# A hybrid decoder step on one core: scores ahead of values, and modulation inside the projections

## The reference, cut to what matters

```python
mod = (silu(c) @ w_ada + b_ada).reshape(B, 6, 1, 1024)          # shift1, scale1, gate1, shift2, scale2, gate2
h = x * (1 + scale1) + shift1
qa, ka, va, qb, kb, vb = split(h @ w_in)                        # six blocks of 512 columns
# rope on q and k; mixer A: 8 heads x 64, dilated windows; mixer B: 4 heads, two maps of 64, values of 128
oa = attend_a(qa, ka, va)                                       # sample: 2048 window rows + 8 new
ob = rms_norm(attend_b(qb, kb, vb, lam), subln_g) * 0.8         # sample: 16 pages of 128 rows + 8 new
x = layer_norm(alpha * x + gate1 * (concat(oa, ob) @ w_o), ...)
h = x * (1 + scale2) + shift2                                   # gated ConvFFN, second layer norm
```

## Time and profile before

| | |
|---|---|
| median of three runs | 1229.12 us |
| lowest and highest | 1226.54 and 1235.38 us |
| the profiled execution | 1233.46 us |
| span of its instructions | 1231.5 us |
| mean granted TensorE clock | 0.923 |
| bytes moved | 276.54 MB |

### The profile page before, as it was taken

One profiled execution on the slowest core, in us unless ns is written; L12 is line 12 of the kernel. 1 busy time (PEld: TensorE's weight loads), 2 busy tenths in 40 slices (PEclk: granted clock), 3 DMA queues, 4 the chain that ended last, 5 costly groups with the idle time before them and its releaser, 6 DMA issues.

```text
span 1231.5 us, 23995 instructions
## 1 busy us (share of the span) xinstructions
PE 1052.7 (85%) x9389; PEld 854.0 (69%) x9389; DVE 839.2 (68%) x1513; ACT 269.5 (22%) x580; POOL 357.9 (29%) x379
## 2 busy tenths in 40 slices
PE   5599999999578677677776996999999999999994
PEld 3377777666455555455555775999999999677772
DVE  1657457167676767667659467567676687998958
ACT  0310010132132223322242104332233222100002
POOL 2333233100000000000016005456565665433323
PEclk9699999999888889778786997999999999999997
DMA  8959895596899999999990215475567731413102
GB/s 303 399 171 327 300 353 174 187 331 220 279 351 344 316 367 322 360 313 343 333 322 1 64 53 195 143 265 207 205 244 274 264 105 69 149 58 106 70 17 77
DMA packets 112549, 276.54 MB, mean 225 GB/s; under 512 B 9608, under 2 KB 33174, under 8 KB 108837
## 3 DMA queue, kind: packets, MB, share of 16 engines
q1 hardware_dynamic: 99125, 250.82, 58.6%
q10 hardware_dynamic: 13312, 24.19, 5.5%
HBM read 264.60 MB, written 76.69 MB: 277 GB/s over the span
## 4 chain that ended last, share of the span: by engine, by line
PE 60%; DVE 18%; DMA 7%; SPq 7%; issue 4%; POOL 2%; ACT 2%; ACTq 0%; DVEq 0%; POOLq 0%; PEldq 0%
PE wide L1576 16%; PE wide L1578 15%; PE wide L1577 15%; DVE ring L1151 3%; PE wide L1650 2%; DMA ring<-in_cache_k 2%; DMA ring<-in_w_ada 2%; PE wide L1639 2%; PE wide L1701 2%; PE wide L1732 2%; DVE ring_r L1083 2%; SPq L598 2%; SPq L433 1%; PE wide L1525 1%; DMA ring<-in_w_down 1%
## 5 line engine op out<-in xcount | busy, mean ns | idle before, releaser
L747 POOL TENSOR_TENSOR ring_r<-ring,ring_r 128x1024 fp32r<-128x1024 f32 x70 | 184.9, 2650 | 271.4 <-DVE ring_r L1043 204.5
L1576 PE MATMUL wide<-x_sb_r,ring_r 128*128 128x288 f32 x704 | 211.4, 300 | 8.2 <-DVE ht_r L1065 5.1
L1577 PE MATMUL wide<-ht_r,ring_r 128*128 128x288 f32 x704 | 209.3, 297 | 0.0
L1578 PE MATMUL wide<-x_sb_r,ring_r 128*128 128x288 f32 x704 | 208.7, 296 | 0.0
L1578 PE MATMUL wide<-ring_r,ht_r 128*128 128x512 f32 (+1 forms) x400 | 158.2, 395 | 0.0
L1151 DVE STREAM_TRANSPOSE ring<-ring 128x512 f32<-128x512 f32 x208 | 129.2, 673 | 20.8 <-DMA ring<-in_cache_k 19.0
L1576 PEld LDWEIGHTS wide<-x_sb_r,ring_r 128*128 128x128 f32 x704 | 133.3, 189 | 11.7 <-issue 11.2
L1578 PEld LDWEIGHTS wide<-x_sb_r,ring_r 128*128 128x128 f32 x704 | 134.2, 191 | 0.0
L1577 PEld LDWEIGHTS wide<-ht_r,ring_r 128*128 128x128 f32 x704 | 133.8, 190 | 0.0
L1576 PE MATMUL wide<-ring_r,x_sb_r 128*128 128x512 f32 (+1 forms) x240 | 97.0, 404 | 10.5 <-DVE ht_r L1065 8.5
L1701 PE MATMUL wide<-ring,x_sb 128*32 128x128 f32 (+1 forms) x1792 | 69.3, 305 | 40.4 <-DVE ring L1151 40.3
(11 more groups left out here) (226 smaller groups left out, 1900.0 us busy)
## 6 DMA issues: line engine op xcount, KB each, us to landing
ring<-in_cache_k SPq DMA_DIRECT2D x128, 256.0 KB
out_wks<-in_cache_win_k SPq DMA_DIRECT2D x8, 4080.0 KB, 19.0
out_wvs<-in_cache_win_v SPq DMA_DIRECT2D x8, 4080.0 KB, 25.3
ring<-in_w_ada SPq DMA_DIRECT2D x12, 2048.0 KB, 10.0
ring<-in_w_up SPq DMA_DIRECT2D x22, 1024.0 KB, 7.6
ring<-in_cache_win_k SPq DMA_DIRECT2D x16, 1024.0 KB
ring<-in_w_in SPq DMA_DIRECT2D x6, 2048.0 KB, 18.4
room<-in_cache_v ACTq DMA_DIRECT2D x32, 256.0 KB
```

The source lines that it names most:

```text
L747: nc.gpsimd.tensor_tensor(rest, w, high.bitcast(F32), ALU.subtract).then_inc(wl_rest, 1)
L1576: nc.tensor.matmul(out, left[0], right[0], start=first, stop=False)
L1577: nc.tensor.matmul(out, left[0], right[1], start=False, stop=False)
L1578: return nc.tensor.matmul(out, left[1], right[0], start=False, stop=last)
```

## The change

**Modulation.** Chunks 4 to 11 leave the weight slots and the prompt attention. Each is loaded into one buffer of its own (`late`, 2 MB in `room`) and computed in the projections ahead of unit 3, 6, 10, 13, 16, 20, 23 and 26; its sum follows one unit later. The window copies of sequences 0 to 3 are no longer issued in pairs at the end of a section but singly, at the units in `COPY_UNIT`.

**Prompt scores.** The queries of the prompt are stored unpadded (`qt`, two heads above each other on 128 partitions); a product contracts over 64 partitions instead of 128 with zeros. POOL no longer zeroes the padded array, and ACT copies a block at once.

**Sample attention.** Within unit w PE first scores all groups of unit w + 1 and its new keys, and then weighs all values of unit w. The scores of the new keys move from bank 4 to bank 7, which the prompt units also use, so that PE waits for the minimum of unit w + 1 before the second prompt step. A prompt step (`prompt_step`) weighs prompt unit y - 2, turns y - 1 and scores y. The raw key buffers move to slot 0 and half of slot 1, so that keys 0 and 1 can be asked for before the projections end; values are loaded only behind the keys of the next unit. ACT issues values 2 and 3 of a mixer B unit and the last key group of a mixer A unit. There is one buffer instead of two for the new rows. The numbers stay: 32 prompt units stand ahead, two in each unit of the sample attention.

```diff
 
-CHUNKS = [("ada", i) for i in range(4)] + [("in", i) for i in range(6)] + [("ada", i) for i in range(4, 12)] \
+CHUNKS = [("ada", i) for i in range(4)] + [("in", i) for i in range(6)] \
...
+
+LATE_UNIT = {4: 3, 5: 6, 6: 10, 7: 13, 8: 16, 9: 20, 10: 23, 11: 26}
+COPY_UNIT = {1: (0, "k"), 4: (0, "v"), 8: (1, "k"), 11: (1, "v"), 14: (2, "k"), 18: (2, "v"), 21: (3, "k"), 24: (3, "v")}
...
+        mod_late = mix[:, 2048:2048 + 2 * CH].rearrange("p (b n) -> p b n", b=2)
+
+        def mod_s(ch):
+
+            return (mod_early if ch < 4 else mod_late)[:, ch % 2, :]
+
+        late = part(room, 12288, KT_D * CH).rearrange("p (k n) -> p k n", k=KT_D)
+        qt = part(room, 0, 4096).rearrange("p (f t) -> p f t", f=8)
+        kt = part(room, 4096, 4096).rearrange("p (f t) -> p f t", f=8)
...
-        kraw = [part(ring, at, 2048).rearrange("p (t d) -> p t d", t=4) for at in (4 * 2048, 5 * 2048, 3 * 2048)]
-        ktg = part(ring, 0, NK * 2048).rearrange("p (b g n) -> p b g n", b=NK, g=16)
+        kraw = [part(ring, at, 2048).rearrange("p (t d) -> p t d", t=4) for at in (0, 2048, 4096)]
+        ktg = part(ring, 6144, NK * 2048).rearrange("p (b g n) -> p b g n", b=NK, g=16)
...
@@ -419,13 +431,27 @@
 
         def values_by_act(w, g):
 
-            return w < len(sa) and w > 0 and (g < 2 if sa[w][0] else g == 1)
-
-        def load_new(eng, w):
+            return sa[w][0] == 1 and g >= 2
+
+        def load_key_tail(eng, w):
+
+            G = NG[w] + 2
+            ks = G % NK
+            if G >= NK:
+                eng.wait_ge(kg_t, G - NK + 1)
...
                 if t == TP:
-                    load_chunk(6 + s)
-                    if s < 3:
-                        move_window(s + 1)
-            for n in range(12, 18):
-                load_chunk(n)
+                    if s < 4:
+                        load_chunk(6 + s)
+                for ch, at in LATE_UNIT.items():
+                    if at == n and ch < 11:
+                        load_late(ch + 1)
+                if n in COPY_UNIT:
+                    i, which = COPY_UNIT[n]
+                    move_window(i, (("cache_win_k", "wks") if which == "k" else ("cache_win_v", "wvs"),))
...
-            load_values(sp, 0, 0)
-            load_values(sp, 0, 1)
-            sp.wait_ge(w_used, CHUNK_AT[("ada", 9)] + 1)
-            group_list = [(w, g) for w, (m, b) in enumerate(sa) for g in range(len(groups[m]))]
...
+            sp.wait_ge(w_used, CHUNK_AT[("in", 4)] + 1)
+
+            def load_keys(w, g):
+
+                m, b = sa[w]
+                G = NG[w] + g
+                ks = G % NK
+                if G >= NK:
+                    sp.wait_ge(kg_t, G - NK + 1)
+                if m == 0:
+                    win_k = flat_k[0][b].rearrange("(g r) h d -> g r (h d)", r=16)
+                    sp.dma_start(kraw[ks][:, :, :], win_k[:, 4 * g:4 * g + 4, :]).then_inc(kg_in[ks], 64)
+                else:
+                    for t, pg in enumerate(page_numbers(sp, b, g)):
+                        sp.dma_start(kraw[ks][:, t, :], flat_k[1][bass.ds(pg, 1)].rearrange("a p h d -> (a p) (h d)"))\
+                            .then_inc(kg_in[ks], 16)
+
+            load_keys(0, 0)
+            load_keys(0, 1)
+            sp.wait_ge(w_used, CHUNK_AT[("in", 5)] + 1)
+            sp.wait_ge(ada_mm, 12)
+            load_key_tail(sp, 0)
+            for w in range(1, len(sa) + 1):
+                here = len(groups[sa[w][0]]) if w < len(sa) else 0
+                if here:
+                    load_keys(w, 0)
+                    load_keys(w, 1)
+                load_values(sp, w - 1, 0)
+                if here == 4:
+                    load_keys(w, 2)
+                load_values(sp, w - 1, 1)
+                if here == 4:
+                    load_keys(w, 3)
+                if sa[w - 1][0] == 0:
+                    load_values(sp, w - 1, 2)
+                if here:
+                    sp.wait_ge(kn_t, w)
+                    load_new_keys(sp, w)
                 if w >= 2:
-                    sp.wait_ge(kn_t, w - 1)
                     sp.wait_ge(sa_pv, w - 1)
-                    load_new(sp, w)
-
...
+            for i, place in enumerate((kn, ktn)):
+                nc.gpsimd.memset(place, 0.0).then_inc(new_zero, 1)
+                pool.wait_ge(new_zero, i + 2)
...
             act.wait_ge(page_in, 16)
+            act.wait_ge(new_zero, 3)
+            act.wait_ge(rope_ok, len(rope_units))
+            act.wait_ge(pj_a, len(v_units))
+            load_new_keys(act, 0)
+            load_new_values(act, 0)
             for u, (m, n, qb) in enumerate(pa[:NU]):
                 act.wait_ge(pa_min, u + 1)
...
 
+                if w + 1 < len(sa) and sa[w + 1][0] == 0:
+                    load_key_tail(act, w + 1)
+                if w:
+                    probs_b(PER * w - 1)
+                    copy_b(PER * w - 2)
+                    take_out(w - 1)
+                if values_by_act(w, 2):
+                    load_values(act, w, 2)
+                probs_b(PER * w)
+                if w:
+                    copy_b(PER * w - 1)
...
-                if values_by_act(w + 1, 0):
-                    load_values(act, w + 1, 0)
-                probs_b(2 * w)
-                if values_by_act(w + 1, 1):
-                    load_values(act, w + 1, 1)
-                if values_by_act(w + 1, 2):
-                    load_values(act, w + 1, 2)
-                copy_b(2 * w)
-                probs_b(2 * w + 1)
-                act.wait_ge(sa_pv, w + 1)
-                nc.scalar.activation(o_s[:, w, :], bk(4)[:, 0:P], ACT.Copy).then_inc(sa_o, 1)
-                copy_b(2 * w + 1)
+                if values_by_act(w, 3):
+                    load_values(act, w, 3)
...
+            jobs += [(n - 0.5, "late_rows", ch) for ch, n in LATE_UNIT.items()]
+            jobs += [(n + 0.55, "late_sum", ch) for ch, n in LATE_UNIT.items()]
...
+                if w:
+                    mask_b(PER * w - 1)
+                    if w >= 2:
+                        out_b(PER * w - 3)
+                if last_g:
+                    turn_keys(w + 1, 1)
+                mask_b(PER * w)
+                if w:
+                    out_b(PER * w - 2)
 
                 full = P * len(groups[m])
                 dve.wait_ge(sa_t, 2 * w + 1)
@@ -1276,19 +1325,15 @@
                 dve.wait_ge(sa_t, 2 * w + 2)
                 nc.vector.tensor_copy(ptn[0:32, :, :], bk(4)[0:32, P:3 * P].rearrange("p (h c) -> p h c", h=2)).then_inc(sa_pt, 1)
                 if last_g:
-                    turn_keys(w + 1, 1)
-                if w:
-                    out_b(2 * w - 1)
-                mask_b(2 * w)
-                if last_g:
                     turn_keys(w + 1, 2)
                 if last_g == 4:
                     turn_keys(w + 1, 3)
-                mask_b(2 * w + 1)
                 if last_g:
                     turn_new(w + 1)
-                out_b(2 * w)
-            out_b(2 * len(sa) - 1)
+            mask_b(len(pb) - 1)
+            out_b(len(pb) - 3)
+            out_b(len(pb) - 2)
+            out_b(len(pb) - 1)
 
             nc.vector.tensor_scalar(rms[:, 0, :], rms[:, 2, :], 1.0 / P, EPS, ALU.mult, ALU.add).then_inc(rms_sq, 1)
...
+                for c, at in LATE_UNIT.items():
+                    if at == n - 1:
+                        ada_sum(c)
+                    if at == n:
+                        ada_rows(c)
...
 
             def prompt_scores(u, bank):
                 m, n, qb = pa[u]
-                return nc.tensor.matmul(bank[:, 0:P * (qb + 1)], qtp[:, 8 * m + n, P * qb:P * qb + P],
-                                        kt[:, 4 * m + n // 2, 0:P * (qb + 1)], start=True, stop=True)
+                at = slice(64 * (n % 2), 64 * (n % 2) + 64)
...
                     pe.wait_ge(pb_o, y)
                 prompt_weigh(NU + y, bk(7)).then_inc(pb_pv, 1)
+
+            def prompt_step(y):
+
+                if y >= 2:
+                    weigh_b(y - 2)
+                if 1 <= y <= len(pb):
+                    turn_b(y - 1)
+                if y < len(pb):
...
-                score(w, 0, bk(4), ktn[:, w % 2], 384, 32)
-                score(w, 1, bk(4), ktn[:, w % 2], 416, 32).then_inc(sa_s, 1)
...
+                if w >= 2:
+                    pe.wait_ge(pb_o, PER * (w - 1) - 1)
+                score(w, 0, bk(7), ktn, 384, 32)
+                score(w, 1, bk(7), ktn, 416, 32).then_inc(sa_s, 1)
...
-                if w:
-                    weigh_b(2 * w - 1)
-                scores_b(2 * w)
-
+                prompt_step(PER * w)
                 for h in range(2):
                     pe.wait_ge(sa_exp, 2 * w + h + 1)
                     if w >= 1:
@@ -1752,31 +1809,31 @@
                     for u in range(len(groups[m])):
                         src = p_tail[:, h, :] if groups[m][u] == 2 else p_s[:, h, P * u:P * u + P]
                         nc.tensor.transpose(bk(2 + h)[:, P * u:P * u + P], src, perm[:, :])
```

(36 more changed lines are left out.)

171 lines of the change are left out of this document (74 added, 97 removed).

## The result

The changed kernel took 1279.26 us in the median of four executions (1263.17 to 1292.76), beside 1232.25 for the kernel before on the same chip. Its ratio is 1.031, 95% interval 1.025 to 1.036, over its two shorter executions (1263.17 and 1271.52). The change costs 3%, and the forecast of 1235, with a range to 1259, was wrong. The profiled execution has a span of 1261.3 us, 29.8 more than the 1231.5 of before.

A forecast was written before the change was run, and what follows sets the result against it. The prediction took PE to bound the projections and DMA transfers the sample attention; 22.9 - 18.9 - 4.7 + 6.2 = +5.5 us gave 1239 for the profiled execution, 1235 us as median, range 1215 to 1259.

The forecast's parts named there:

- Part 2: Prompt attention without modulation: 6.4 us per four units instead of 8.77, -18.9 us; bounds -22.5 and -14.
- the half clock as an extra in the sample stage: Sample attention: half clock adds to the slower, starving case; a score group took 1.94 us against 1.08.
- Part 1: Projections: eight modulation chunks of 2.86 us move in, PE has no hole to hide them, +22.9 us.
- The rival of late loads: Projections: late modulation loads arrive late because DMA keeps to 252 GB/s; 10 us taken, 1245 us, chance 10%.
- 3 to 6 us of slack each: Projections: spare time counted for each late modulation load, so 0 us taken for waiting.
- Part 3: Hand-over to sample attention: new rows asked for earlier, -4.7 us; value loads no longer hidden, +6.2 us.
- the tail: End of sample attention: two prompt units after the last values, claimed to be as now.
- The lost prefetch: Hand-over: 2.1 MB of value loads, hidden under modulation before, come into the transfer-bound stage, +6.2 us.
- Part 4: Sample attention, all scores then values: PE path 37 us a pair, under 40.2 of transfers, so 0 us.
- just inside the bound I had set: Sample attention: the forecast counts as wrong if a pair of units moves by over 1.5 us either way.
- The rival of starving transfers: Sample attention: value buffers come free in a burst, DMA idles 2 to 4 us a pair, +24, 1259 us, chance 25%.
- The fast rival: Sample attention: transfers are not the bound, a pair goes down to 37 us, -30, 1205 us, chance 12%.

The follow-up runs named there:

- e6: Changed kernel with 128-row prompt score products (adds up two heads, so that part computes something else): 1250.58 us, ratio 1.017.
- e1: Kernel before with one edit, prompt score products over 64 rows instead of 128: 1240.90 us, ratio 1.009.
- e10: Changed kernel with 128-row score products in the first four prompt units alone (these add up two heads): 1255.33 us, ratio 1.019.
- e12: Changed kernel with the load of modulation chunk 7 moved ahead of a w_in chunk and a value store in SP's list: 1280.64 us median, too scattered for a ratio.
- r1: Changed kernel run once more without edit: 1255.61, 1269.20, 1293.06 and 1293.33 us.
- e9: Kernel before with the changed sample order, last values ahead of w_o, and first new rows asked for before the prompt exps, in small single buffers: 1231.56 us, ratio 1.000.
- e11: Changed kernel with four repairs (dense burst, last values ahead of w_o, first two value groups and first key turns moved into prompt attention): 1242.71 us, ratio 1.010.
- e2: Changed kernel with the last sample unit's value groups 2 and 3 issued by SP ahead of the w_o weights: 1253.44 us, ratio 1.020.
- e5: Kernel before with only the changed sample attention order, and the last values issued ahead of w_o: 1231.21 us, ratio 1.001.
- e3: Changed kernel with ACT issuing the first new rows before prompt unit 12 instead of before unit 0: 1256.71 us, ratio 1.022.
- e7: Changed kernel with a burst of 16 dense, unused products on PE behind the fourth prompt unit: 1257.87 us, ratio 1.022.

## Why the prediction was wrong, step by step

**Part 2 failed, in one clause.** The pace was sized well: 64.3 - 18.9 = 45.4 us between the first and the last mask, and e6 took 45.8, though not for the reason given: I had DVE at 90% beside PE, and from 280 to 310 us e6 shows PE busy 98% and DVE 82%. But that is the time with 128-row products. The clause was that 64 rows instead of 128 "change no column count, so the score product stays at its price". A column count prices a product alone; the price here is in the neighbours, whose weight load no longer runs under it. That is +7.3 us (e1; e6 against e10), and the range had no bound for it, since I looked for the product's duration and not for what starts during it. PE is the bound in this stage with either kind of product, and with the longer ones DVE falls from 82 to 75% of it.

**The second half of that term is the clock.** I took the 1.00 of the earlier trace rows over into a stage whose work was to change. From the 53.1 us that 32 units take in 64 rows at full clock (45.8 + 7.3) to the 66.5 measured, 13.4 us are, by difference, half clock in the profiled execution; with 55.1 it is 2.0 in the best and with 91.0 it is 37.9 in the worst. Together 7.3 + 13.4 = 20.7, and the term was missed by 21.1. I named the half clock as an extra in the sample stage, where PE waits a good deal and loses little; the stage in which PE is the bound was the place.

**Part 1 was right but for its slack.** +22.9 forecast, +25.7 measured. In that, 4.8 us are one late chunk, and 2.3 are taken off by the start: the first product comes 5.8 us earlier than before (50.7 against 56.5), after a second wait and more products at half clock the fifteenth still comes 2.3 earlier (59.2 against 61.5). What is left is 23.2, for 22.9 forecast. The rival of late loads happened in small: one load in eight was late, by 4.5 to 6.1 us, in each of the ten traces that have the change's projections (in e6 a second one by under 1 us). The "3 to 6 us of slack each" counted the bytes ahead of a load; it left out that SP's list waits, here for the rotated keys until 129.5, so that a w_in chunk and the load went out together (e12). With that load in front, the next was late.

**Part 3 and the tail, right in sum for a poor reason.** Forecast -4.7 + 6.2 + 0 = +1.5, measured +0.5, and +3.9 in r1, whose stretch is 341.1 us; that the sum fits is luck, for its terms do not. The gap before the first min chain shrank by 4.2 us, as forecast, but by e9 part of that is paid ahead of it, in the wait of PE for the first exp, which I had put at a bound of 1 us and at nothing in the sum; there the last mask came 2.0 us later and the end moved by nothing. The lost prefetch may be real, since e11, with it and more, is 16.6 us shorter here, 6 to 9 us beyond what e2's order brings; its 6.2 was not measured alone. "The tail is as now" was wrong: 15.0 us became 30.0, of which 8 to 11 are w_o beside the last values (e2), and the rest fits the earlier chains, whose other side it is in e5 (24.5 us there).

**Part 4 held**, as far as these runs test it. DMA share 0.98 at 345 GB/s; PE waits for turned keys (45.8 us in all), 23.8 us for values and only 4.5 for exp; chains 19.67 us apart instead of 20.36, a pair 1.4 us shorter, just inside the bound I had set; and e5 finds the order, together with that of the last values, worth nothing, as forecast. The rival of starving transfers did not happen. The fast rival neither: the stage did reach 373 GB/s for 60 us,

```profile
460.00:520.00 60.00, 42.77 (x849) 32.02 (x852) 42.59 (x104) 15.22 (x51) 2.31 (x8) 0.83 1.04 373
```

but over 300 us it held 345, where before had 339.

**What stays open.** Why the clock falls with 64-row products and not with 128-row ones is not settled. They differ in the rows of the array that work and in the holes between product and weight load, and no run here parts the two. The wait at the start may help the fall along, but e3 fell without it. Why the clock comes back by itself after 7 us in one execution, 31 in another and 92 in a third isn't known either. The 1.4 us behind the sums were not looked into: before, e1 and e5 take 590.6 to 591.3 us there, e9 and all kernels with the change 592.1 to 593.3. Why the late load moves on when one is brought forward isn't shown (e12). Why e2, without prefetched values, is 7 us shorter from last mask to sums than e5 with them (329.8, 336.7) was not looked into; the pace and the key turns at the end of their prompt attentions differ.

## What to carry to other kernels

Taking rows out of a product was not free here, where its neighbours kept theirs: look at what is loaded under it before costing it at nothing. When dense work leaves a stage in which PE is the bound, the stage's clock is no longer known, and the first few products can then decide over much of it (e7, e10); price it at both levels. In a stage bound by transfers count the bytes left to its last landing, not the chains: in e5 a mark moved by 10 us and the end by none. And when a wait survives the edit that was to remove it, look whether it is still the same wait.

## What the runs showed of the hardware that I had not expected

A matmul over 64 rows between matmuls over 128 delays the next weight load to its end (0.84 us after its start instead of 0.32), at 7.3 us in 32 units. The granted clock depends on such products: the same wait of PE at the start, 1.34 to 1.36 us, was followed by 0.50 in after and by 1.00 in e6 and e10, which differ from it in the rows of 32 and of 4 units' score products; in e3 the 0.50 came without that wait. The Trainium skill, TensorE: Matmul & The Clock Gate, HAM oscillation, ties the fall to waits of PE between its products; here the same wait led to both levels. And the lower level can last: 7 to 92 us, in which PE, once past the wait, never showed idle, ended in e7 within a burst of 5.8 us of dense products. Of two 2 MB loads issued within 1.1 us of each other on SP's queue the first landed after 8 us and the second after 13 to 14.5, whichever it was (after, e12).
